# Weight-block sums of a seven-product feed-forward layer, moved from GpSimd additions to accumulating DMAs

## The chip, the cores and the metric

The kernel runs on one core of a Trainium2 chip. The metric is the device time of one execution in microseconds (us); lower is better. The engines are named PE (TensorE), ACT (ScalarE), DVE (VectorE), POOL (GpSimd) and SP (SyncE, which here issues loads).

## The reference, cut to what matters

One step of a hybrid backbone of four layers: each layer is a token mixer (short convolution, pooling, attention, short convolution) followed by a SwiGLU feed-forward part, all in float32, over 512 sample tokens and 128 prompt tokens with a model width of 1024. The part that the change touches is the feed-forward part of the last layer:

```python
D_FF = 2816
def swiglu(h, w_in, w_out):
    g, u = jnp.split(h @ w_in, 2, axis=-1)
    return (jax.nn.silu(g) * u) @ w_out
...
for i in range(DEPTH):
    ...
    hp = modulate(rms_norm(xp, norm2_w[i]), mod_p[3], mod_p[4])
    hs = modulate(rms_norm(xs, norm2_w[i]), mod_s[3], mod_s[4])
    xp = xp + mod_p[5] * swiglu(hp, ffn_in_w[i], ffn_out_w[i])
    xs = xs + mod_s[5] * swiglu(hs, ffn_in_w[i], ffn_out_w[i])
```

## The kernel before

Features lie on the 128 partitions and the 640 tokens on the free axis. Float32 products are made of three passes: a matrix is split into a high half (ACT copies it to float32r) and a low half (DVE subtracts the high half from the original), and PE adds hi x hi, hi x lo and lo x hi. Weights come in units of 128 output columns, 128 x 1024 elements (512 KB), into the four buffers `raw[:, 0..3]`. The split halves go to `w_hi` and `w_lo`, which hold two units each.

**The feed-forward part.** The 22 output tiles of `w_in` come in pairs, a gate unit and an up unit. They are worked on in three chunks of 8, 8 and 6 pairs, and behind each chunk stand two quads of units of `w_out` (the out quads). In layers 0 to 2 a pair is plain: two units, eight blocks of 128 rows of weight each. In layer 3 all pairs but the first two of the first chunk go through seven products in place of eight half-size ones, so the chunks hold 6, 8 and 6 such pairs, 20 in all. The pair is a 2 x 2 matrix of blocks: gate and up, each with the half of the weight rows that meets features 0 to 511 (here "gate half 0", "up half 0") and the half that meets the others (half 1). The tokens' 640 columns are cut into two halves too. A product is 12 matmuls (4 blocks of 128 rows x 3 passes) of 128 x 322 columns, the two extra columns carrying the shift of the modulation. The products' weight blocks, by number:

- 1: gate half 0; 2: gate half 1; 4: up half 1, as loaded
- 5: S1 = up half 0 + up half 1
- 7: S3 = gate half 0 - up half 0
- 6: S2 = S1 - gate half 0
- 3: S4 = gate half 1 - S2

Against them stand token sums T1 to T4 (`t1_hi` and so on), which POOL makes once for the layer ("turned rows"), ACT and DVE split, and all 20 pairs use. The results are added up in PSUM and by DVE (`c11`, `c12`: gate; `c21`, `c22`: up).

**What sets the order.** Each engine has one program in a fixed order with semaphores between. The products run in the order of `_order`: for pair p, product 1, then product 4 of pair p-1, then 5, 6, 2, 7, 3. `w_hi` and `w_lo` hold four blocks. When a product is done, ACT splits the block that goes to its place, four products ahead (`block_hi`, line 1250), and DVE follows (`block_lo`, line 1818). ACT also copies results out of PSUM (product 1 at line 1289, product 5 at 1296, product 6 at 1300), applies Silu (1310) and splits the hidden rows (1315). The last of a pair's blocks to be split is block 4, and its low half frees the pair's two raw buffers (line 1822, the mark). Raw buffers 0 and 1 hold even pairs, 2 and 3 odd pairs, so a pair's load begins once the pair two ahead of it is split.

**The sums before.** POOL makes the four sums of a pair with `tensor_tensor` in this order: S1 into `s1_home`, a row of `tmp` (line 591); S3 in place over up half 0, when block 1 has been split (595); S2 in place over gate half 0 (601); S4 in place over gate half 1, when block 2 has been split (608). SP's program has one loop of raw loads for the quads (`load`, line 443). The feed-forward part of layer 3 begins with one plain quad (PE lines 701 and 702; DVE line 1785 multiplies its gate and up rows), while POOL makes the turned rows.

Of the kernel before, what the change touches and what calls it, by code (L numbers as in the profile page):

```python
# [26 lines left out]
KD = D // P  # L27
# [145 lines left out]
def build(nc, d):  # L173
    with ExitStack() as ctx:
# [99 lines left out]
        s_made = sem("s_made")  # L274
# [146 lines left out]
        def _(sp):  # L421
# [58 lines left out]
            for layer in range(DEPTH):  # L480
# [33 lines left out]
                with sp.Fori(0, 2 * (Q_IN + Q_OUT)) as i:  # L514
                    load(i + q, KD)
                q += 2 * (Q_IN + Q_OUT)
                with sp.Fori(0, Q_LAST) as i:
                    load(i + q, KD)
                q += Q_LAST
# [11 lines left out]
        def _(pool):  # L531
# [45 lines left out]
            def s13(layer, c, p, q, n):  # L577

                first, j, qq = _pairs_before(layer, c), 2 * (p % 2), q + p // 2
# [3 lines left out]
                if p == 0 and c == 0:  # L583

                    pool.wait_ge(sum_ready, 2 * layer + 2)
                elif p:

                    pool.wait_ge(block_lo_ready, SEVEN * first + PLACE[n][p - 1, 5] + 1)
                elif c > FIRST_SEVEN[layer]:
                    pool.wait_ge(block_lo_ready, SEVEN * first)  # L590
                pool.tensor_tensor(s1_home, up_w[:, 0:HW], up_w[:, HW:2 * HW], ALU.add).then_inc(s_made, 1)

                pool.wait_ge(block_lo_ready, SEVEN * first + PLACE[n][p, 1] + 1)
                pool.wait_ge(s_made, 4 * (first + p) + 1)
                pool.tensor_tensor(up_w[:, 0:HW], gate_w[:, 0:HW], up_w[:, 0:HW], ALU.subtract).then_inc(s_made, 1)

            def s2(layer, c, p):
                first, gate_w = _pairs_before(layer, c), raw[:, 2 * (p % 2), :]

                pool.wait_ge(s_made, 4 * (first + p) + 2)  # L600
                pool.tensor_tensor(gate_w[:, 0:HW], s1_home, gate_w[:, 0:HW], ALU.subtract).then_inc(s_made, 1)

            def s4(layer, c, p, n):
                first, gate_w = _pairs_before(layer, c), raw[:, 2 * (p % 2), :]

                pool.wait_ge(block_lo_ready, SEVEN * first + PLACE[n][p, 2] + 1)
                pool.wait_ge(s_made, 4 * (first + p) + 3)
                pool.tensor_tensor(gate_w[:, HW:2 * HW], gate_w[:, HW:2 * HW], gate_w[:, 0:HW], ALU.subtract).then_inc(s_made, 1)

            def begin_chunk(layer, c, q, n):  # L610

                s13(layer, c, 0, q, n)
                s2(layer, c, 0)
                s4(layer, c, 0, n)

            def rest_of_chunk(layer, c, q, n, triples):

                for p in range(1, n):
                    if p % 2 == 1 and p > 1 and p // 2 < len(triples):
# [12 lines left out]
            for layer in range(DEPTH):  # L632
# [34 lines left out]
                for c in range(FIRST_SEVEN[layer], 3):  # L667
                    tiles = SEVENS[c]
                    qc = q + c * (Q_IN + Q_OUT) + (PLAIN_PAIRS // 2 if c == 0 else 0)
                    triples = [t0 + per * c + i for i in range(tiles // 2)] if ada and c < 2 else []  # L670
                    if layer == 0 and c == 2:
                        triples = [t0 + 2 * per]
                    begin_chunk(layer, c, qc, tiles)
                    if triples and not (kind == "attn" and c == 0):
                        ada_triple(triples[0])
                    rest_of_chunk(layer, c, qc, tiles, triples)
# [520 lines left out]
        def _(act):  # L1197
# [43 lines left out]
            def block_hi(n, b, first, q):  # L1241

                p, m = ORDER[n][b]
                if m in (1, 2):
                    act.wait_ge(raw_in[2 * (p % 2)], 16 * (q + p // 2) + 16)
                elif m == 4:
                    act.wait_ge(raw_in[2 * (p % 2) + 1], 16 * (q + p // 2) + 16)
                else:
                    act.wait_ge(s_made, 4 * (first + p) + {5: 1, 7: 2, 6: 3, 3: 4}[m])
                act.activation(block_home(w_hi, n, b), block_source(p, m), ACT.Copy).then_inc(block_hi_ready, 1)  # L1250
# [6 lines left out]
            def t1_hi_of(layer, k):  # L1257
                act.wait_ge(t1_made, HALF * LAYER_T[layer] + k + 1)
                act.activation(t1_hi[:, k, :], t2_full[:, k, :], ACT.Copy).then_inc(t_hi_ready, 1)

            def t2_hi_of(layer, k):
                act.wait_ge(t2_made, HALF * LAYER_T[layer] + k + 1)
                act.activation(t2_hi[:, k, :], t2_full[:, k, :], ACT.Copy).then_inc(t_hi_ready, 1)
# [4 lines left out]
            def t4_hi_of(layer, k):  # L1268
                act.wait_ge(t4_made, HALF * LAYER_T[layer] + k + 1)
                act.wait_ge(t_lo_ready, T_STEPS * LAYER_T[layer] + 2 * HALF + k + 1)  # L1270
                act.activation(t4_hi[:, k, :], t4_full[:, k, :], ACT.Copy).then_inc(t_hi_ready, 1)
# [422 lines left out]
        def _(dve):  # L1694
# [134 lines left out]
            def t1_lo_of(layer, k):  # L1829
                dve.wait_ge(t_hi_ready, T_STEPS * LAYER_T[layer] + k + 1)  # L1830
                dve.tensor_tensor(t1_lo[:, k, :], t2_full[:, k, :], t1_hi[:, k, :].bitcast(F32), ALU.subtract).then_inc(t_lo_ready, 1)

            def t2_lo_of(layer, k):
# [3 lines left out]
                dve.tensor_tensor(t2_lo[:, k, :], t2_full[:, k, :], t2_hi[:, k, :].bitcast(F32), ALU.subtract).then_inc(t_lo_ready, 1)  # L1837
# [5 lines left out]
            def t4_lo_of(layer, k):  # L1843
                dve.wait_ge(t_hi_ready, T_STEPS * LAYER_T[layer] + 3 * HALF + k + 1)
                dve.tensor_tensor(t4_lo[:, k, :], t4_full[:, k, :], t4_hi[:, k, :].bitcast(F32), ALU.subtract).then_inc(t_lo_ready, 1)

            def seven_chunk(layer, c, q, n, pr, g, tiles, ada):
# [49 lines left out]
                def after_p7(p):  # L1897
# [702 lines left out]
```

## Time and profile before

| | us |
|---|---|
| median of 3 runs (2642.04 to 2642.1) | 2642.05 |
| the profiled execution | 2642.6 |
| its span, first to last instruction | 2640.9 |
| PE busy (99% of the span) | 2624.2 |
| DVE busy (70%) | 1852.4 |
| ACT busy (34%) | 888.4 |
| POOL busy (10%) | 251.2 |

The busy share of PE counts a matmul from its start to its modelled end, and matmuls overlap, so 99% says that PE rarely stands still, not that it runs at its peak. The profile gives, for each idle stretch of an engine, what released it; a timeline gives instructions in order of time, and neighbours that are alike are merged. The seven-product chunks of layer 3 and the out quads between them lie from 2217 us to the end of the span.

### The profile page before, as it was taken

To read this page: it belongs to the slowest core of one execution; us is meant where nothing else is said; L and a number is where in the kernel's file an instruction comes from. 1 tells how busy PE (TensorE), PEld (TensorE's weight loads), DVE (VectorE), ACT (ScalarE), POOL (GpSimd) and SP (SyncE) were. 2 spreads that over 40 slices of the span, in tenths; PEclk is the share of its full clock that TensorE was granted. 3 is DMA by queue.
4 is the path that set the end of the run, shared out by engine and by line. 5 is a ranking of instruction groups with operands and counts; after the bars stand their busy time and mean duration, and the time that the engine had idled before them with its cause. 6 is when DMAs were issued, how large, how long until landed. Compare 5 with 4: busy or idle time off the path is not lost.

```text
span 2640.9 us, 45052 instructions
## 1 busy us (share of the span) xinstructions
PE 2624.2 (99%) x17398; PEld 2553.1 (97%) x17398; DVE 1852.4 (70%) x3097; ACT 888.4 (34%) x1330; POOL 251.2 (10%) x297
## 2 busy tenths in 40 slices
PE   9999999999999999999999999999999999999998
PEld 5999999999999999999967999999999999999998
DVE  5888778676586776846676668768465558849486
ACT  4223331222342222124675432221242234425253
POOL 0000000000000000000000000000000026224040
PEclk9999999999999999999999999999999999999999
DMA  8444435444224454522101245444222221312222
GB/s 308 146 143 139 132 127 175 130 156 143 77 77 128 152 158 127 152 71 75 56 13 73 82 126 162 149 127 152 69 82 72 72 79 49 104 57 90 86 76 77
DMA packets 85625, 295.19 MB, mean 112 GB/s; under 512 B 10112, under 2 KB 13312, under 8 KB 85248
## 3 DMA queue, kind: packets, MB, share of 16 engines
q1 hardware_dynamic: 60016, 200.74, 23.5%
q0 software_dynamic: 25488, 92.81, 11.4%
q8 instruction: 79, 1.29, 0.2%
q14 instruction: 42, 0.34, 0.0%
HBM read 290.63 MB, written 2.88 MB: 111 GB/s over the span
## 4 chain that ended last, share of the span: by engine, by line
PE 92%; DVE 4%; issue 1%; ACT 1%; DMA 1%; DVEq 0%; ACTq 0%; SPq 0%
PE ps L701 40%; PE ps L702 40%; PE ps L754 6%; PE ps_x L1000 1%; PE ps_sum L754 1%; PE ps L976 1%; DVE w_lo L1818 1%; PE ps_sum L987 1%; PE ps L1132 1%; DMA mix<-in_ada_head 1%; DVE w_lo L1698 1%; PE ps L1083 0%; PE ps L857 0%; ACT w_hi L1200 0%; DVE tmp L1913 0%
## 5 line engine op out<-in xcount | busy, mean ns | idle before, releaser
L1698 DVE TENSOR_TENSOR w_lo<-raw,w_hi 128x1024 fp32r<-128x1024 f32 (+2 forms) x319 | 382.3, 1198 | 464.8 <-ACT w_hi L1200 463.5
L1200 ACT ACTIVATE w_hi<-raw 128x1024 fp32r<-128x1024 f32 (+2 forms) x319 | 329.3, 1032 | 917.8 <-PE ps L702 905.8
L701 PE MATMUL ps<-h_hi,w_hi 128*128 128x320 f32 x1568 | 490.2, 313 | 1.2 <-DVE h_lo L2011 0.7
L702 PE MATMUL ps<-h_lo,w_hi 128*128 128x322 f32 x1568 | 488.5, 312 | 0.0
L701 PE MATMUL ps<-h_lo,w_hi 128*128 128x320 f32 x1568 | 487.3, 311 | 0.0
L702 PE MATMUL ps<-h_hi,w_lo 128*128 128x322 f32 x1568 | 487.3, 311 | 0.0
L701 PE MATMUL ps<-h_hi,w_lo 128*128 128x320 f32 x1568 | 487.0, 311 | 0.0
L702 PE MATMUL ps<-h_hi,w_hi 128*128 128x322 f32 x1568 | 486.0, 310 | 0.0
L1726 DVE CUSTOM_DVE_ANT_0 ps_x<-ada_w,cond 128x1024 f32<-128x1024 f32 x354 | 435.9, 1231 | 33.5 <-DVE tmp L1774 12.9
L701 PEld LDWEIGHTS ps<-h_hi,w_hi 128*128 128x128 f32 x1568 | 295.6, 189 | 2.4 <-DVE h_lo L2011 0.8
L702 PEld LDWEIGHTS ps<-h_hi,w_hi 128*128 128x128 f32 x1568 | 297.2, 190 | 0.6
L702 PEld LDWEIGHTS ps<-h_hi,w_lo 128*128 128x128 f32 x1568 | 297.3, 190 | 0.0
L701 PEld LDWEIGHTS ps<-h_hi,w_lo 128*128 128x128 f32 x1568 | 296.5, 189 | 0.0
L702 PEld LDWEIGHTS ps<-h_lo,w_hi 128*128 128x128 f32 x1568 | 295.6, 189 | 0.0
L701 PEld LDWEIGHTS ps<-h_lo,w_hi 128*128 128x128 f32 x1568 | 294.4, 188 | 0.0
L701 PE MATMUL ps<-g_hi,w_hi 128*128 128x320 f32 x884 | 274.3, 310 | 0.4
L702 PE MATMUL ps<-g_hi,w_lo 128*128 128x320 f32 x884 | 273.2, 309 | 0.0
L701 PE MATMUL ps<-g_hi,w_lo 128*128 128x320 f32 x884 | 273.1, 309 | 0.0
L702 PE MATMUL ps<-g_lo,w_hi 128*128 128x320 f32 x884 | 273.1, 309 | 0.0
L702 PE MATMUL ps<-g_hi,w_hi 128*128 128x320 f32 x884 | 273.1, 309 | 0.0
L701 PE MATMUL ps<-g_lo,w_hi 128*128 128x320 f32 x884 | 273.1, 309 | 0.0
L542 POOL DMA_DIRECT2D ada_w<-in_ada_w x177 | 93.6, 529 | 1730.4 <-DVE ada_raw L1726 1352.1
(237 smaller groups left out, 4090.9 us busy)
## 6 DMA issues: line engine op xcount, KB each, us to landing
raw<-in_weights SPq DMA_DIRECT2D x323, 512.0 KB, 3.5
ada_w<-in_ada_w POOLq DMA_DIRECT2D x177, 512.0 KB, 3.8
raw<-in_weights SPq DMA_DIRECT2D x32, 384.0 KB, 3.0
mix<-in_ada_head SPq DMA_DIRECT2D x16, 512.0 KB, 10.5
x<-in_x SPq DMA_DIRECT2D x8, 320.0 KB, 10.1
out_y<-mix SPq DMA_DIRECT2D x16, 160.0 KB, 1.9
mix<-in_spread SPq DMA_DIRECT2D x1, 1088.0 KB, 5.4
cond<-in_cond SPq DMA_DIRECT2D x1, 1024.0 KB, 13.6
```

The costliest lines, as they stand in the source:

```text
L542: pool.dma_start(ada_w[:, j * D:(j + 1) * D], d["ada_w"][ADA_N * qa + (j - LEAD)]).then_inc(ada_in[j], 16)
L701: pe.matmul(ps[:, 2 * slot, 0:TA], w[:, slot, ws], a(k)[:, 0:TA], start=begin, stop=end)
L702: mm = pe.matmul(ps[:, 2 * slot + 1, 0:width - TA], w[:, slot, ws], a(k)[:, TA:width], start=begin, stop=end)
L754: mm = pe.matmul(out, w[:, ws], a[:, k, :], start=begin and k == 0 and i == 0, stop=k == HALF - 1 and i == 2, skip_group_check=True)
L976: pe.matmul(out[:, 0:TS], row[:, qt * P:(qt + 1) * P], key[:, 0:TS], start=True, stop=True)
L987: mm = pe.transpose(sum_flat[:, k * P:(k + 1) * P], tmp[:, n % 2, k * P:(k + 1) * P], ident[:])
L1000: pe.matmul(ps_rot, val, of_sample[:, k, :], start=(k == 0), stop=(k == 4))
L1132: mm = pe.matmul(head_row[g % 2], cond_k[:, 2 * pair + k, :], head_w[:, n % HEAD_SLOTS, k * HEAD_W * P:(k + 1) * HEAD_W * P], start=(pair ...
L1200: act.activation(w_hi[:, j % 2, 0:tiles * P], raw[:, j, 0:tiles * P] if src is None else src, ACT.Copy).then_inc(w_hi_ready, 1)
L1698: dve.tensor_tensor(w_lo[:, j % 2, 0:tiles * P], raw[:, j, 0:tiles * P] if src is None else src, w_hi[:, j % 2, 0:tiles * P].bitcast(F32), ...
L1726: dve.tensor_tensor_reduce(ada_products, ada_w[:, j * D:(j + 1) * D], cond[:, v, :], 1.0, 0.0, ALU.mult, ALU.add, ada_raw[:, j, v:v + 1]). ...
L1818: dve.tensor_tensor(block_home(w_lo, n, b), block_source(p, m), block_home(w_hi, n, b).bitcast(F32), ALU.subtract).then_inc(block_lo_ready, 1)
```

## The change

The four sums of a pair are no longer made by POOL's arithmetic but by DMAs that POOL issues and that add their source to what lies at the destination. S1, S2 and S4 get places of their own: `s1_home` and `s2_home` in `rope` (a table that only the attention of layer 2 uses) and `s4_home` in the row of `tmp` where S1 was. SP loads each with one operand straight from the weights in DRAM (256 KB each), and POOL's DMA adds the other:

- S3 over up half 0: += gate half 0
- S1: loaded with up half 0, += up half 1
- S2: loaded with up half 1, += S3
- S4: loaded with gate half 1, += S2

A DMA of this kind only adds, so the up half is carried with the other sign. T1, T2 and T4 are negated when they are split (ACT `Identity` with scale -1, DVE a two-operation instruction), DVE multiplies the up results by -1 along with their scale, and the shift is subtracted where it was added. Gate half 0 and gate half 1 are no longer overwritten. SP's program for layer 3 is written out pair by pair: two raw loads, then the three homes, each with its waits. A home is reloaded when the low half of the block made from it has been split; S2's home also waits for S4 of the pair before, which reads it; and `s4_home` of the first pair waits for `sum_ready`, which SP waits for now and POOL did before. POOL's waits for raw loads stay; its waits for splits are replaced by waits for the homes and for S3 and S2. ACT waits for four semaphores of DMAs (which count 16 for each) where it waited for one that counted POOL's additions.

```diff
-        s1_home = tmp[:, 2, 0:HW]
+        s1_home, s2_home, s4_home = rope[:, 0, 0:HW], rope[:, 1, 0:HW], tmp[:, 2, 0:HW]
...
-            return {1: raw[:, j, 0:HW], 6: raw[:, j, 0:HW], 2: raw[:, j, HW:2 * HW], 3: raw[:, j, HW:2 * HW],
-                    7: raw[:, j + 1, 0:HW], 4: raw[:, j + 1, HW:2 * HW], 5: s1_home}[m]
+            return {1: raw[:, j, 0:HW], 2: raw[:, j, HW:2 * HW], 4: raw[:, j + 1, HW:2 * HW], 7: raw[:, j + 1, 0:HW],
+                    5: s1_home, 6: s2_home, 3: s4_home}[m]
...
+            def load_pair(layer, c, q, p):
+                first, place, j, qq = _pairs_before(layer, c), PLACE[SEVENS[c]], 2 * (p % 2), q + p // 2
+                load(qq, KD, (j, j + 1))
+                gate_w, up_w = d["weights"][4 * qq + j], d["weights"][4 * qq + j + 1]
+                def free(m):
+                    if p:
+                        sp.wait_ge(block_lo_ready, SEVEN * first + place[p - 1, m] + 1)
+                    elif first:
+                        sp.wait_ge(block_lo_ready, SEVEN * first)
+                free(5)
+                sp.dma_start(s1_home, up_w[:, 0:HW]).then_inc(s1_in, 16)
+                free(6)
+                if first + p:
+                    sp.wait_ge(s4_made, 16 * (first + p))
+                sp.dma_start(s2_home, up_w[:, HW:2 * HW]).then_inc(s2_in, 16)
+                free(3)
+                if p == 0 and c == FIRST_SEVEN[layer]:
+                    sp.wait_ge(sum_ready, 2 * layer + 2)
+                sp.dma_start(s4_home, gate_w[:, HW:2 * HW]).then_inc(s4_in, 16)
...
-            def s13(layer, c, p, q, n):
...
-                pool.tensor_tensor(s1_home, up_w[:, 0:HW], up_w[:, HW:2 * HW], ALU.add).then_inc(s_made, 1)
...
-                pool.tensor_tensor(up_w[:, 0:HW], gate_w[:, 0:HW], up_w[:, 0:HW], ALU.subtract).then_inc(s_made, 1)
...
+            def sums_of_pair(layer, c, p, q):
+                made, j, qq = 16 * (_pairs_before(layer, c) + p + 1), 2 * (p % 2), q + p // 2
+                gate_w, up_w = raw[:, j, :], raw[:, j + 1, :]
                 pool.wait_ge(raw_in[j], 16 * qq + 16)
                 pool.wait_ge(raw_in[j + 1], 16 * qq + 16)
+                pool.dma_start(up_w[:, 0:HW], gate_w[:, 0:HW], accum_op=ALU.add).then_inc(s3_made, 16)
+                pool.wait_ge(s1_in, made)
+                pool.dma_start(s1_home, up_w[:, HW:2 * HW], accum_op=ALU.add).then_inc(s1_made, 16)
+                pool.wait_ge(s3_made, made)
+                pool.wait_ge(s2_in, made)
+                pool.dma_start(s2_home, up_w[:, 0:HW], accum_op=ALU.add).then_inc(s2_made, 16)
+                pool.wait_ge(s2_made, made)
+                pool.wait_ge(s4_in, made)
+                pool.dma_start(s4_home, s2_home, accum_op=ALU.add).then_inc(s4_made, 16)
...
-                act.activation(t1_hi[:, k, :], t2_full[:, k, :], ACT.Copy).then_inc(t_hi_ready, 1)
+                act.activation(t1_hi[:, k, :], t2_full[:, k, :], ACT.Identity, scale=-1.0).then_inc(t_hi_ready, 1)
...
-                    dve.tensor_tensor(up_row(p)[:, TA:T], up_row(p)[:, TA:T], rinv[:, TA:T], ALU.mult).then_inc(up_scaled, 1)
+                    dve.scalar_tensor_tensor(out=up_row(p)[:, TA:T], in0=up_row(p)[:, TA:T], scalar=-1.0, in1=rinv[:, TA:T],
+                                             op0=ALU.mult, op1=ALU.mult).then_inc(up_scaled, 1)
...
-                                                     op0=ALU.add, op1=ALU.mult)
+                                                     op0=ALU.subtract, op1=ALU.mult)
```

POOL's program at the first seven-product pair of layer 3, before: the four sums of pair 0 and the first of pair 1 (`tmp` holds S1; `raw_in0` to `raw_in3` are the raw loads).

```order
L591 TENSOR_TENSOR tmp<-raw 128x512 [waits sum_ready,raw_in1,raw_in0]
L595 TENSOR_TENSOR raw<-raw 128x512 [waits s_made,block_lo_ready]
L601 TENSOR_TENSOR raw<-tmp,raw 128x512 [waits s_made]
L608 TENSOR_TENSOR raw<-raw 128x512 [waits s_made,block_lo_ready]
L591 TENSOR_TENSOR tmp<-raw 128x512 [waits block_lo_ready,raw_in3,raw_in2]
```

The same place after: S3, S1, S2 and S4 of pair 0 and S3 of pair 1, all as DMAs.

```order
L626 DMA raw<-raw 128x512 [waits raw_in1,raw_in0]
L628 DMA rope<-raw 128x512 [waits s1_in]
L632 DMA rope<-raw 128x512 [waits s2_in,s3_made]
L636 DMA tmp<-rope 128x512 [waits s4_in,s2_made]
L626 DMA raw<-raw 128x512 [waits raw_in3,raw_in2]
```

S3 moved ahead of S1, and no sum waits for a split any more; S4 stands ahead of the next pair's S3.

SP's program where the feed-forward part of layer 3 begins, before: the loop of raw loads.

```order
L514 UNCONDITIONAL_BRANCH
L514 ISA
L443 ISA [waits w_lo_ready]
L443 DMA raw<-in_weights 128x1024
L442 REGISTER_ALU
```

SP's program after, from the first seven-product pair on: pair 0, then pair 1 (`rope` is the home of S1 and then of S2, `tmp` that of S4).

```order
L449 DMA raw<-in_weights 128x1024 [waits w_lo_ready] x2
L464 DMA rope<-in_weights 128x512
L469 DMA rope<-in_weights 128x512
L474 DMA tmp<-in_weights 128x512 [waits sum_ready]
L449 DMA raw<-in_weights 128x1024 [waits w_lo_ready] x2
L464 DMA rope<-in_weights 128x512 [waits block_lo_ready]
L469 DMA rope<-in_weights 128x512 [waits s4_made,block_lo_ready]
L474 DMA tmp<-in_weights 128x512 [waits block_lo_ready]
```

Between the raw loads of two pairs there now stand three loads that wait for splits, and one of them waits for S4 of the pair before.

## Rows read from the trace of the kernel before

**Rows 1.** PE's waits, 2040 to 2641 us: total, times, longest

```profile
PE ps L754 <- ACT tmp L1289: 2.6, 1, 2.6
...
PE ps L754 <- DVE tmp L1901: 0.5, 1, 0.5
PE ps L701 <- DVE w_lo L1698: 0.4, 1, 0.4
```

**Rows 2.** windows: length, busy of PE, PEld, DVE, ACT, POOL; clock, DMA share, GB/s

```profile
2226.00:2227.00 1.00, 1.00 (x6) 1.00 (x5) 1.00 (x3) 1.00 (x3) 0.00 (x0) 0.50 0.00 0
2235.00:2236.00 1.00, 1.00 (x9) 1.00 (x8) 1.00 (x3) 1.00 (x3) 0.00 (x0) 1.00 0.02 4
2426.10:2438.95 12.85, 12.70 (x85) 12.44 (x84) 12.78 (x18) 6.83 (x13) 5.91 (x4) 1.00 0.24 82
2438.95:2451.80 12.85, 12.77 (x87) 12.51 (x86) 12.21 (x22) 6.41 (x12) 2.90 (x2) 1.00 0.34 107
```

**Rows 3.** timeline of PE: start, length, line, output<-inputs, instructions merged, idle before

```profile
2225.47 0.90 PE L754 MATMUL ps<-turned,w_hi 128*128 128x322 f32 x2 [2.59 <-ACT tmp L1289]
...
2228.65 0.31 PE L754 MATMUL ps<-h_hi,w_hi 128*128 128x322 f32 x1
...
2234.70 0.57 PE L754 MATMUL ps<-turned,w_hi 128*128 128x322 f32 x2 [0.53 <-DVE tmp L1901]
```

**Rows 4.** timeline of DVE ahead of and in the first chunk

```profile
2207.95 1.01 DVE L1785 SCALAR_TENSOR_TENSOR tmp<-tmp,bias 128x512 f32<-128x512 f32 x2
...
2220.36 2.17 DVE L1785 SCALAR_TENSOR_TENSOR tmp<-tmp,bias 128x512 f32<-128x512 f32 x2
...
2232.48 1.77 DVE L1818 TENSOR_TENSOR w_lo<-tmp,w_hi 128x512 fp32r<-128x512 f32 x1
```

**Rows 5.** timeline of ACT, the same stretch

```profile
2210.98 0.61 ACT L1250 ACTIVATE w_hi<-tmp 128x512 fp32r<-128x512 f32 x1
...
2222.56 0.74 ACT L1212 ACTIVATE g_hi<-tmp 128x640 fp32r<-128x640 f32 x1 [3.84 <-DVE tmp L1785]
...
2225.01 0.41 ACT L1289 ACTIVATE tmp<-ps 128x320 f32<-128x320 f32 x1
```

**Rows 6.** timeline of POOL, the same stretch

```profile
2204.75 1.29 POOL L591 TENSOR_TENSOR tmp<-raw 128x512 f32<-128x512 f32 x1
...
2220.63 1.74 POOL L591 TENSOR_TENSOR tmp<-raw 128x512 f32<-128x512 f32 x1
...
2231.95 1.75 POOL L601 TENSOR_TENSOR raw<-tmp,raw 128x512 f32<-128x512 f32 x1
```

**Rows 7.** DMA issues, median us to landing (x5: 2364 to 2390 us); line 542

```profile
raw<-in_weights SPq DMA_DIRECT2D x323, 512.0 KB, 3.5
ada_w<-in_ada_w POOLq DMA_DIRECT2D x177, 512.0 KB, 3.8
...
raw<-in_weights SPq DMA_DIRECT2D x4, 256.0 KB, 2.5
...
raw<-in_weights SPq DMA_DIRECT2D x5, 512.0 KB, 4.2
...
L542 POOL DMA_DIRECT2D ada_w<-in_ada_w x177: 527/527/697, 36.4 to 1824.7; - x177
```

**Rows 8.** timelines of DVE, then ACT, in the steady part of the second chunk

```profile
2375.18 0.06 DVE L1822 MEMSET marks<- 128x1 f32 x1
...
2377.91 0.69 DVE L1818 TENSOR_TENSOR w_lo<-tmp,w_hi 128x512 fp32r<-128x512 f32 x1
...
2375.20 0.63 ACT L1250 ACTIVATE w_hi<-tmp 128x512 fp32r<-128x512 f32 x1 [1.14 <-PE ps L754]
...
2387.70 0.63 ACT L1250 ACTIVATE w_hi<-tmp 128x512 fp32r<-128x512 f32 x1 [1.14 <-PE ps L754]
2389.48 0.63 ACT L1250 ACTIVATE w_hi<-raw 128x512 fp32r<-128x512 f32 x1 [1.15 <-PE ps L754]
...
2395.36 0.63 ACT L1250 ACTIVATE w_hi<-raw 128x512 fp32r<-128x512 f32 x1 [1.10 <-POOL raw L608]
```

More of the change, by code:

```diff
@@ L273, in build @@
         t_lo_ready = sem("t_lo_ready")
-        s_made = sem("s_made")
+        s1_in = sem("s1_in")
+        s2_in = sem("s2_in")
+        s4_in = sem("s4_in")
+        s1_made = sem("s1_made")
+        s2_made = sem("s2_made")
+        s3_made = sem("s3_made")
+        s4_made = sem("s4_made")
         block_hi_ready = sem("block_hi_ready")
@@ L513, in _ @@
                 q += Q_MIX[kind]
-                with sp.Fori(0, 2 * (Q_IN + Q_OUT)) as i:
+                plain = min(FIRST_SEVEN[layer], 2) * (Q_IN + Q_OUT)
+                if FIRST_SEVEN[layer] == 0:
+                    plain += PLAIN_PAIRS // 2
+                with sp.Fori(0, plain) as i:
                     load(i + q, KD)
[L516 to L519, printed above, removed]
+                q += plain
+                for c in range(FIRST_SEVEN[layer], 3):
+                    for p in range(SEVENS[c]):
+                        load_pair(layer, c, q, p)
+                    q += SEVENS[c] // 2
+                    if c < 2:
+                        with sp.Fori(0, Q_OUT) as i:
+                            load(i + q, KD)
+                        q += Q_OUT
+                if FIRST_SEVEN[layer] == 3:
+                    with sp.Fori(0, Q_LAST) as i:
+                        load(i + q, KD)
+                    q += Q_LAST
                 with sp.Fori(0, Q_OUT) as i:
@@ L582, in s13 @@
                 pool.wait_ge(raw_in[j + 1], 16 * qq + 16)
[L583 to L590, printed above, removed]
-                pool.tensor_tensor(s1_home, up_w[:, 0:HW], up_w[:, HW:2 * HW], ALU.add).then_inc(s_made, 1)
-                pool.wait_ge(block_lo_ready, SEVEN * first + PLACE[n][p, 1] + 1)
@@ L594, in s13 @@
-                pool.wait_ge(s_made, 4 * (first + p) + 1)
-                pool.tensor_tensor(up_w[:, 0:HW], gate_w[:, 0:HW], up_w[:, 0:HW], ALU.subtract).then_inc(s_made, 1)
[L597 to L619, printed above, removed]
+                pool.dma_start(up_w[:, 0:HW], gate_w[:, 0:HW], accum_op=ALU.add).then_inc(s3_made, 16)
+                pool.wait_ge(s1_in, made)
+                pool.dma_start(s1_home, up_w[:, HW:2 * HW], accum_op=ALU.add).then_inc(s1_made, 16)
@@ new lines, in sums_of_pair, with sums_of_chunk @@
+                pool.wait_ge(s3_made, made)
[4 more added lines that the diff above has]
+                pool.dma_start(s4_home, s2_home, accum_op=ALU.add).then_inc(s4_made, 16)
+            def sums_of_chunk(layer, c, q, n, triples):
+                for p in range(n):
+                    if p % 2 == 1 and p // 2 < len(triples):
@@ L620, in rest_of_chunk @@
                         ada_triple(triples[p // 2])
-                    s13(layer, c, p, q, n)
-                    s2(layer, c, p)
-                    s4(layer, c, p, n)
+                    sums_of_pair(layer, c, p, q)
             def turn_rows(layer):
@@ L672, in _ @@
                         triples = [t0 + 2 * per]
[L673 to L676, printed above, removed]
+                    sums_of_chunk(layer, c, qc, tiles, triples)
                     if ada and c < 2:
@@ L1248, in block_hi @@
                 else:
-                    act.wait_ge(s_made, 4 * (first + p) + {5: 1, 7: 2, 6: 3, 3: 4}[m])
+                    act.wait_ge({5: s1_made, 6: s2_made, 7: s3_made, 3: s4_made}[m], 16 * (first + p + 1))
                 act.activation(block_home(w_hi, n, b), block_source(p, m), ACT.Copy).then_inc(block_hi_ready, 1)
```

17 lines of the change are left out of this document (10 added, 7 removed).

## The prediction, made before the run

> **What bounds the kernel now.** I read the page's busy shares first, then TensorE's (PE's) waits in layer 3's feed-forward part, then the other engines around each wait. PE is busy for 99% of the span, so the change can win back only the little time in which PE stands still, while nothing bounds what it can lose. In the 600 us that hold everything the change touches, PE waits for little: 2.6 us once for ScalarE (ACT) and 0.5 us once for VectorE (DVE) inside the seven-product code (line 754), and 0.4 us in the plain unit ahead of it [rows 1]. The 2.6 us wait costs more than its length: the product behind it ran at a granted clock of 0.50, that is at 1.2 instead of 2.4 GHz [rows 2], and its twelve matmuls took from 2225.47 to 2228.65, 3.18 us [rows 3], where a product takes 12.50 / 7 = 1.79 us (the hi of S1 recurs every 12.50 us, 2375.20 to 2387.70 [rows 8], and a pair is seven products). So the clock cost 1.4 us more.
>
> Why did PE wait? Product 6 of pair 0 needs the copy of product 1 that ACT makes at 2225.01 (line 1289), and ACT stood behind a DVE product that ended at 2222.5 [rows 5]. That DVE step (line 1785, two instructions) took 2.17 us; the same two took 1.01 us at 2207.95 [rows 4]. In between, GpSimd (POOL) was adding S1 of pair 1, from 2220.63 for 1.74 us [rows 6]. The same shows at the second wait: a low half (line 1818) took 1.77 us at 2232.48 against 0.69 us at 2377.91 [rows 4, 8], beside a POOL addition at 2231.95 of 1.75 us [rows 6]. DVE and POOL hold each other up.
>
> In the steady part DVE is full: 12.78 us of a 12.85 us stretch, where PE idles 0.15 us, and 0.08 us in the stretch behind [rows 2]. PE there still lives on blocks split ahead, and the loop of DVE and POOL is a little slower than PE.
>
> **What the change gives back.** All 80 additions leave POOL's compute. POOL still makes the turned rows T1 to T4 until 2204.75, where its first S1 begins now [rows 6], so what PE lost before that stays.
> - The step at line 1785: 2.17 - 1.01 = 1.16 us. Everything behind it on ACT until line 1289 is a chain, so product 6 starts 1.16 us sooner. The rest of that wait, 2.59 - 1.16 = 1.43 us, stays.
> - The clock: it fell after 2.59 us of idle time, and in the stretch behind 0.53 us of idle it reads 1.00 [rows 2, 3]. 1.43 us is nearer to 0.53 than to 2.59, so I take the clock as kept: 1.40 us. Its ends are 0 and 1.40.
> - The second wait, 0.53 us [rows 3]: the DVE step ahead of it loses 1.77 - 0.69 = 1.08 us, more than the wait. All of it: 0.53 us.
> - The thin idle time in the second chunk: 0.15 + 0.08 = 0.23 us [rows 2], gone once DVE has spare time.
> Sum: 1.16 + 1.40 + 0.53 + 0.23 = 3.32 us.
>
> **What it adds beside other work.** ACT's scaled copies replace plain ones, one for one. DVE gets eight two-operation forms for T1 and T2, four for T4 and 40 for the up half, in place of plain additions and products. A two-operation form on 128x512 plus one on 128x128 takes 1.01 us [rows 4], so these are no longer than what stands now, within about 0.1 us; they lie in a DVE that loses POOL's hindrance. SP issues 60 more loads of 256 KB, and POOL 80 accumulating DMAs. None of these is on PE's path as long as each sum is there when ACT splits it. That is the point on which all hangs, so here is its room.
>
> **The room, from the steady part.** Pair P's raw blocks may be loaded once the low half of block 4 of pair P-2 is made (the mark at 2375.18 [rows 8]). Two loads of 512 KB, 4.2 us in the median there [rows 7] and one behind the other, are in by about 2380.5. POOL then issues S3 and S1. S1's home is reloaded after the low half of S1 of P-1 (2377.91 + 0.69 = 2378.6) and in 2.5 us later, 2381.1 [rows 7, 8]. ACT wants S1 at 2387.70, S2 at 2389.48 and S4 at 2395.36 [rows 8].
> - S1: 2387.7 - 2381.1 = 6.6 us for one accumulation that runs beside S3.
> - S2 behind S3: 2389.5 - 2380.5 = 9.0 us for two, 4.5 us each. This is the tightest.
> - S4 behind both: 14.9 us for three, 5.0 us each.
> - The ring: S4 of P-1 frees S2's home, which SP reloads (2.5 us), then S2, then S4 of P. That is 2.5 + 2B for an accumulation of B us, against 12.50: B up to 5.0 us.
> A late sum makes ACT wait, and behind it stand its evacuations of PE's banks; on SP the next pair's raw loads stand behind the new wait for S4; on POOL the next pair's S3 and S1 behind the waits for S2 and S4. Below B = 4.5 us nobody waits; from 5.0 the delay adds up pair by pair. Pair 0 has room: S3 and S1 can go at 2204.75, so at 3.8 us each S1 is in by about 2209.6 (ACT splits it at 2210.98 [rows 5]) and S2 by 2212.9, before ACT's turn to split it after 2217.
>
> **What an accumulation costs.** No row shows one. From below: 256 KB land in 2.5 us from SP, and POOL's queue is 0.3 us slower than SP's for 512 KB (3.8 against 3.5), so 2.8 us [rows 7]. From above: a sum reads two operands and writes one, 768 KB of movement; 512 KB cost 1.0 us more than 256 KB, so at worst 2.8 + 2 x 1.0 = 4.8 us. I take 3.8 us, the row of POOL's own 512 KB DMA, since the two operands that are read are 512 KB. With 3.8 us nobody waits. The neighbours' loads could add to it: the engines now move 1.75 MB of loads and 1 MB of sums per pair, where rows show a share of 0.24 for 1 MB [rows 2]; counting each sum twice that is 0.24 x 3.75 = 0.90 of the DMA engines. That is full enough to be my main doubt.
>
> One rule speaks against the change. The rows show POOL issuing its 177 ada loads in 527 ns each and never over 697 [rows 7], with DVE busy for 70% of the span. The Trainium skill, page "SBUF — State Buffer", section "A bandwidth-pool intuition that's wrong (but worth ruling out)", says that a DMA issued by GpSimd can stand still while DVE holds the port through which its descriptors are written, and gives 620 ns alone against 3100 ns beside a DVE copy. By that an accumulation would be an estimated 2.5 us longer, 6.3 us, and past the ring's limit. The trace's issues do not agree with it for the DVE work in them; what stands beside the new DMAs is other DVE work.
>
> **The rivals.**
> 1. *The ring closes (slower).* If B is over 5.0 us, each pair takes 2.5 + 2B. At B = 6.0: 14.5 us, 2.0 us over, for 7 + 5 + 5 = 17 intervals of the chunks of 8, 6 and 6 pairs: 34 us. Blocks are split three products ahead, 3 x 1.79 less 1.3 us for the two halves, about 4 us of cushion in each of three chunks: 34 - 12 = 22 us, less the 3.3 gained: 2642.05 + 19 = 2661 us. For it: crowded engines, three sums in series. Against: the estimate of 3.8.
> 2. *POOL's issue is held up by DVE (slower).* Each issue waits for up to one DVE step, 2.17 us at most here [rows 4]: B = 3.8 + 2.2 = 6.0, again 2661 us. Against: the 697 ns. This is the case of the Trainium skill's page above.
> 3. *The relief does not come (no change).* The DVE steps are long for another reason, or what ends last is then ACT: first and second waits stay, 2642 us.
> 4. *The waits go altogether.* All of 2.59 + 1.40 + 0.53 + 0.23 = 4.75 us and something of the plain unit's 0.4 [rows 1], with more restart time than I counted: 2636.5 us.
>
> **How the numbers follow.** The profiled execution took 2642.6 us, with 1.7 us outside the 2640.9 us span and 0.55 us over the median of the runs; the gain is taken from the median: 2642.05 - 3.32 = 2638.7 us. Its own range, with the clock's 1.4 us lost at one end and the first wait gone at the other, is 2637.0 to 2640.5. Chances: forecast 50%; relief absent, or small waits that eat the gain (B of 4.5 to 5.0), 17%; ring 24%; held issue 5%; all waits gone 4%. A measurement of this kernel can tell 0.2%, 5.3 us, from no change. So faster is the last case alone, 0.04; slower the ring and the held issue, 0.29; the rest, 0.67, is within 0.2%. The range reaches to a B of just over 6 us, 2664 us, which leaves out some 14% above and a few below.
>
> **What would show it.** Right: the accumulations land in under 4.5 us; DVE's line 1785 step ahead of the chunk takes about 1.0 us, PE's first wait there about 1.4 us and the granted clock stays at 1.00; DVE falls well under 12 us per pair; no wait of ACT for a sum. Wrong: landings over 5 us with ACT's high halves waiting for DMAs, and chunks whose pairs take longer than 12.5 us, most of it in the chunk of eight.

## The result, and the profile after

The changed kernel took 2671.37 us in the median, against 2642.07 us for the kernel before on the same chip: a ratio of 1.011 with a 95% interval of 1.0097 to 1.0122, or 29.3 us more. The forecast was 2638.7 us, the range ended at 2664 us. The direction was that of the first rival, "the ring closes".

Line numbers have moved: PE's products of the seven-product code are line 771 (was 754), ACT's high halves line 1267 (1250), its copies of product 1 line 1306 (1289), DVE's low halves line 1835 (1818), the product step ahead of the chunk line 1802 (1785). The sums are POOL's lines 626 (S3), 628 (S1), 632 (S2) and 636 (S4), SP's home loads lines 464 (S1), 469 (S2) and 474 (S4), its weight loads line 449.

The page of the changed kernel: busy time and share of each engine, then the DMA queues (q1 is SP's, q0 POOL's) with the share of 16 engines, then the chain that ended last, by engine.

```profile
PE 2632.0 (99%) x17398; PEld 2558.6 (96%) x17398; DVE 1801.5 (67%) x3097; ACT 884.5 (33%) x1330; POOL 199.4 (7%) x297
...
q1 hardware_dynamic: 68656, 216.48, 25.1%
q0 software_dynamic: 37008, 113.79, 15.8%
...
PE 87%; DMA 6%; DVE 3%; issue 2%; ACT 2%; POOL 0%; DVEq 0%; SPq 0%; ACTq 0%; POOLq 0%
```

DVE and POOL lost some 50 us of work each, as planned. But the chain of work that ended last now holds 6% of DMA. PE's waits (total, times, longest), 2040 us to the end, say where:

```profile
PE ps L771 <- DVE w_lo L1835: 22.9, 11, 4.4
PE ps L771 <- ACT tmp L1306: 1.4, 1, 1.4
```

The second row is the first wait of before [rows 1], shorter, as forecast. The first row is new: eleven waits for a low half. All eleven stand between products 5 and 6 of a pair: PE waits for S2. Six of them, 14.4 us, lie in the chunk of eight. The stretch in the middle of the chunk of eight pairs shows it against before. Columns: length, busy time of PE, PEld, DVE, ACT and POOL, granted clock, DMA share, GB/s. The kernel before:

```profile
2380.00:2460.00 80.00, 79.78 (x536) 79.16 (x535) 76.82 (x110) 42.11 (x78) 30.83 (x21) 1.00 0.26 88
```

The changed kernel:

```profile
2380.00:2460.00 80.00, 68.91 (x440) 67.73 (x439) 48.58 (x90) 33.28 (x66) 18.10 (x21) 0.96 0.78 187
```

PE stands still for 11 of 80 us here; DVE, 96% full before, is at 61%. The DMA engines went from 0.26 to 0.78.

**How one wait comes about.** Timelines of the changed kernel (start, length, idle time before and what ended it), POOL's and SP's issues in that stretch, then ACT, DVE and PE at the end of the same sum:

```profile
2405.24 0.84 POOL L636 DMA_DIRECT2D tmp<-rope  x1 [5.03 <-DMA rope<-raw]
2405.78 1.19 POOL L626 DMA_DIRECT2D raw<-raw  x1
2406.31 1.52 POOL L628 DMA_DIRECT2D rope<-raw  x1
2413.25 0.85 POOL L632 DMA_DIRECT2D rope<-raw  x1 [5.41 <-DMA rope<-in_weights]
2419.68 0.84 POOL L636 DMA_DIRECT2D tmp<-rope  x1 [5.58 <-DMA rope<-raw]
...
2408.64 0.33 SPq L469 DMA_DIRECT2D rope<-in_weights  x1
...
2412.39 0.81 SPq L449 DMA_DIRECT2D raw<-in_weights  x2
...
2419.48 0.63 ACT L1267 ACTIVATE w_hi<-rope 128x512 fp32r<-128x512 f32 x1 [6.71 <-DMA rope<-raw]
...
2420.14 0.69 DVE L1835 TENSOR_TENSOR w_lo<-rope,w_hi 128x512 fp32r<-128x512 f32 x1 [4.26 <-ACT w_hi L1267]
...
2420.98 0.53 PE L771 MATMUL ps<-turned,w_hi 128*128 128x322 f32 x2 [1.75 <-DVE w_lo L1835]
```

Each length here runs from one issue to the issue that it releases. S4 of one pair goes out at 2405.24. It frees the S2 home, which SP reloads at 2408.64, 3.4 us later. The reload is in by 2413.25, after 4.6 us, and at that moment POOL, which had waited 5.41 us for it, issues S2. S2 is in at 2419.68, after 6.4 us. There the next S4 goes out, and ACT, DVE and PE follow one after the other; PE had stood still for 1.75 us. The three members make 3.4 + 4.6 + 6.4 = 14.4 us a pair, where PE needs 12.5 us. This is the ring of the prediction, and it is longer than a pair. The pair shown is one of the shorter ones: from the second S2 of this chunk (issued at 2363.68) to the last (2458.41) they stand 12.7 to 18.4 us apart, 15.8 us in the mean.

**What the waits cost.** The clock goes with them. The changed kernel's windows in which the granted clock is below 1.00 in its seven-product chunks:

```profile
2270.00:2295.00 25.00, 21.38 (x133) 20.90 (x132) 13.59 (x25) 10.30 (x20) 5.14 (x6) 0.93 0.75 179
...
2380.00:2400.00 20.00, 15.65 (x96) 15.41 (x95) 10.88 (x21) 7.33 (x14) 4.09 (x5) 0.91 0.73 163
...
2420.00:2440.00 20.00, 16.56 (x101) 16.36 (x102) 12.73 (x24) 9.61 (x21) 5.73 (x7) 0.91 0.77 171
...
2460.00:2480.00 20.00, 16.72 (x97) 16.48 (x96) 10.90 (x23) 6.95 (x13) 0.84 (x1) 0.83 0.45 124
...
2580.00:2600.00 20.00, 17.99 (x111) 17.76 (x110) 13.36 (x26) 10.18 (x20) 3.98 (x5) 0.91 0.85 192
```

Each holds one of the five longest waits, 2.0 to 4.4 us; part of the work behind it ran at 1.2 GHz. By these rows 0.07 x 25 + 3 x 0.09 x 20 + 0.17 x 20 = 10.6 us of clock are missing. Some of that is counted in the waits already: from 2467 to 2468 us the granted clock is 0.50 while PE is busy for 0.25 us. In finer windows PE works for 18.6 us at 1.2 GHz in these five stretches, and half of that, 9.3 us, is what the clock costs. With the 22.9 us of waits it makes 32.2 us; the gains take off 3.3, and 28.9 us remain, where 29.3 were measured.

**The gains came too.** DVE's step ahead of the chunk, PE's product behind the first wait, and the product before which the second wait stood, in the changed kernel's timelines:

```profile
2220.27 1.01 DVE L1802 SCALAR_TENSOR_TENSOR tmp<-tmp,bias 128x512 f32<-128x512 f32 x2
...
2224.23 0.56 PE L771 MATMUL ps<-turned,w_hi 128*128 128x322 f32 x2 [1.44 <-ACT tmp L1306]
...
2231.81 0.56 PE L771 MATMUL ps<-turned,w_hi 128*128 128x322 f32 x2
```

The window around the second of them:

```profile
2223.00:2227.00 4.00, 2.77 (x19) 2.77 (x20) 4.00 (x9) 4.00 (x11) 0.45 (x1) 1.00 0.49 83
```

2.17 us became 1.01, the first wait 1.44 instead of 2.59 us, the granted clock behind it 1.00 (2.4 GHz) instead of 0.50, and the second wait is gone [rows 2 to 4].

### The profile page after: what moved, and what is told of

Its sections match the earlier page's. It is cut to its first block, busy times and chain, and to the rows that moved or that the text cites. A ratio compares the mean times of both kernels' runs of the same rounds, so it can differ in the third digit from the quotient of the medians.

```text
span 2670.5 us, 44991 instructions
## 1 busy us (share of the span) xinstructions
PE 2632.0 (99%) x17398; PEld 2558.6 (96%) x17398; DVE 1801.5 (67%) x3097; ACT 884.5 (33%) x1330; POOL 199.4 (7%) x297
## 3 DMA queue, kind: packets, MB, share of 16 engines
q0 software_dynamic: 37008, 113.79, 15.8%
q8 instruction: 79, 1.29, 0.2%
## 4 chain that ended last, share of the span: by engine, by line
PE 87%; DMA 6%; DVE 3%; issue 2%; ACT 2%; POOL 0%; DVEq 0%; SPq 0%; ACTq 0%; POOLq 0%
PE ps L718 39%; PE ps L719 39%; DMA rope<-raw 2%; PE ps L771 2%; DMA rope<-in_weights 2%; PE ps_x L1017 1%; PE ps L993 1%; DMA raw<-in_weights 1%; PE ps_sum L1004 1%; PE ps L1149 1%; DMA tmp<-rope 1%; DMA mix<-in_ada_head 1%; DVE w_lo L1715 1%; PE ps_sum L771 0%; DVE w_lo L1835 0%
```

## The experiments

Two theories had to be told apart. **The ring**: one S2 home, freed by S4 and reloaded, ties each pair's S2 to the S4 before. **The load**: full DMA engines make every transfer slow, whatever waits for what. A third, POOL's issue held up by DVE, was a rival too.

**1. Is it the sums' cost at all?** Two kernels keep every instruction, wait and queue and make the sums cheaper. One sums half the columns of each block (so its sums are incomplete), the other copies instead of adding (so the blocks are not sums):

```diff
-pool.dma_start(s2_home, up_w[:, 0:HW], accum_op=ALU.add)
+pool.dma_start(s2_home[:, 0:HW // 2], up_w[:, 0:HW // 2], accum_op=ALU.add)   # half sums, all four
+pool.dma_start(s2_home, up_w[:, 0:HW])                                        # plain copies, all four
```

> Every accumulating DMA adds only the first 256 of 512 columns, so half of each sum is left out; waits, homes and loads are as in the changed kernel. Ring theory: each sum loses its share of the traffic, S2 falls from 6.4 to about 4.5 us and the reload from 4.6 to 3.6, the ring to 11.5 us, under 12.5, so 2638 to 2646 us. Full-engines theory: engine time per pair falls from 10.6 to 7.6 us, also 2638 to 2646 us; the two differ in the run with two homes, not here. Held-issue theory: the issues are as many and as long, about 2671 us.

> The four DMAs of a pair copy instead of adding (so no sum is made), same queue, shapes, homes and waits. It measures what the addition costs. If reading the destination doubles a sum's traffic, a copy costs 0.7 us of the engines where a sum costs 1.5, lands in 2.8 us alone, and the ring falls to about 11.5 us: 2638 to 2646 us. If a sum is slow for its way through the queue and not for its addition, copies land in the 5 to 6 us of the sums and the time stays near 2670 us.

Measured: 2638.66 us with half sums (ratio 0.9988, 0.9978 to 0.9997) and 2638.52 us with copies (0.9987, 0.9978 to 0.9996). Both stand at the forecast, 2638.7. The rest of the change is worth what the sum said, and all of the loss lies in what the four accumulations cost. The DMA view of 2040 to 2600 us (queue: packets, MB, share of 16 engines; issues: count, KB, median us to landing), for the changed kernel:

```profile
q0 software_dynamic: 11232, 20.45, 22.0%
...
rope<-in_weights SPq DMA_DIRECT2D x40, 256.0 KB, 4.1
rope<-raw POOLq DMA_DIRECT2D x40, 256.0 KB, 5.5
```

for the kernel with copies:

```profile
q0 software_dynamic: 6400, 20.98, 10.1%
...
rope<-in_weights SPq DMA_DIRECT2D x40, 256.0 KB, 3.5
rope<-raw POOLq DMA_DIRECT2D x40, 256.0 KB, 2.6
```

The window holds the packets of 78 sums (a 79th is issued there, but the last S2, issued at 2599.44, moves its bytes behind it: 20.45 MB are 78 times 256 KB) or of 80 copies. A sum takes 0.220 x 560 / 78 = 1.58 us of all 16 engines, a copy of the same 256 KB 0.101 x 560 / 80 = 0.71 us: 2.2 times as much. In the kernel with half sums POOL's issues of S2 take 0.85 to 0.88 us, as in the changed kernel, and the time is back, so POOL's issue is not what is late. (A copy's issue takes 0.54 us.)

**2. Cut the ring, keep the bytes.** A second S2 home in a tile that is free in this layer, taken in turn; the reload then waits for S4 of the pair before the last:

```diff
-sp.wait_ge(s4_made, 16 * (first + p))
-sp.dma_start(s2_home, up_w[:, HW:2 * HW]).then_inc(s2_in, 16)
+sp.wait_ge(s4_made, 16 * (first + p - 1))
+sp.dma_start(s2_homes[p % 2], up_w[:, HW:2 * HW]).then_inc(s2_in[p % 2], 16)
```

> S2 gets two homes, one for even and one for odd pairs (the second in the modulation-weight buffer, idle in layer 3); its reload waits for S4 of the pair two before instead of the pair before. Nothing else is changed, the same bytes move. Ring theory (S4 of a pair, 3.4 us, then the reload of S2's home, 4.6 us, then S2, 6.4 us: 14.4 us against 12.5 us per pair): the ring is cut, PE's waits for late S2 go, the time falls to 2638 to 2643 us. Full-engines theory (a sum costs 1.5 us of all 16 DMA engines, with the loads 10.6 us per pair of 12.5, and what is full stays full): the bytes are the same, S2 still ends late, 2660 us or more. Held-issue theory (POOL's issues wait for DVE): nothing changes, about 2671 us.

Measured: 2647.15 us, ratio 1.0021 (1.001 to 1.0031). Some 24 of the 29 us are back with every transfer still made. PE's waits, 2217 to 2640 us:

```profile
PE ps L774 <- DVE w_lo L1838: 3.5, 1, 3.5
PE ps L774 <- ACT tmp L1309: 1.4, 1, 1.4
PE ps L774 <- ACT tmp L1320: 1.2, 1, 1.2
```

Eleven waits for a low half have become one. But 8.5 us over the kernels with cheap sums stay. The two waits that are left beside the first lie at 2253 and 2553 us, at the third pair of the first chunk and the fourth of the last.

A wider cut, two homes for each of S1, S2 and S4, asks whether more lead removes this rest:

> The changed kernel with two homes for each of S1, S2 and S4, taken in turn, and all four accumulating DMAs and all home loads kept: same bytes, twice the lead for every home. Theory A, the bytes: the DMA engines still carry 10.6 us of each 12.5 us pair, transfers still land after 4 to 6 us, and more lead for the loads removes only part: 2641 to 2650 us, about as with two S2 homes alone (2647.15 us). Rival B, lead is all that lacks: the loads run one pair ahead, every sum is made early, and the time is the 2638.5 us of the kernels with cheap sums.

Measured: 2648.18 us, ratio 1.0029 (1.002 to 1.0039). It does not. Loading homes earlier gave nothing more here once the ring was cut.

**3. Move the meeting.** In the ring, the next pair's 1 MB of weights (2412.39) goes out just ahead of S2 (2413.25). Was that meeting the cause? The loads were put behind S2 of the pair before, in the kernel with one S2 home:

```diff
+if first + p:
+    sp.wait_ge(s2_made, 16 * (first + p))
 load(qq, KD, (j, j + 1))
```

and, with two homes, behind S2 of the second pair before.

> The changed kernel, one S2 home and the ring as they are, all bytes and all sums as they are; the only edit: the two 512-KB weight loads of a pair wait until S2 of the pair before has landed, so that they no longer run beside it (in the changed kernel they start within 1 us of S2's issue in each pair of the ring, and S2 then takes 6.4 us). Theory A, this meeting of two transfers is what stretches the ring: S2 lands after 3.3 to 4 us, the loads meet S4 instead, which then takes longer than its 3.4 us but is in the ring too; the period falls from 14.4 us by about 2 us to at most 12.5 us, and the time to 2640 to 2652 us. Rival B, the engines carry a fixed sum of work in a period and what S2 gains S4 and the reload lose: 2662 to 2675 us. Rival C, the weights come too late for S3 of the next pair, and the ring grows a longer way round: over 2675 us.

> The variant with two S2 homes (2647.15 us), with one more edit: the two 512-KB weight loads of a pair wait until S2 of the second pair before has landed, since in its profile S2 took 8.2 us where 1 MB of weights was issued 1.2 us ahead of it. Theory A, the meeting of the weight loads with S2 makes what is left over the 2638.5 us of the kernels with cheap sums: the waits of 1.3 and 3.7 us on TensorE go, 2638.5 to 2642 us. Rival B, the sums that start a chunk are late by the order of their own chain, and the loads only move to another meeting: 2645 to 2650 us.

Measured: 2670.49 us (1.009 to 1.0121) with one home, 2647.29 us (1.0011 to 1.0029) with two. Neither moved: my theory fell, and each time lies in the range of rival B. Timelines of POOL and SP in the kernel with one home:

```profile
2387.05 0.85 POOL L638 DMA_DIRECT2D tmp<-rope  x1 [2.72 <-DMA rope<-raw]
...
2398.41 0.85 POOL L634 DMA_DIRECT2D rope<-raw  x1 [1.61 <-DMA rope<-in_weights]
2402.14 0.85 POOL L638 DMA_DIRECT2D tmp<-rope  x1 [2.88 <-DMA rope<-raw]
...
2386.78 0.81 SPq L449 DMA_DIRECT2D raw<-in_weights  x2
...
2395.58 0.33 SPq L471 DMA_DIRECT2D rope<-in_weights  x1
```

S2 now takes 2402.14 - 2398.41 = 3.7 us and the reload 2.8 us. But S4, which meets the weights instead, takes 2395.58 - 2387.05 = 8.5 us until SP can reload. The sum is 15.0 us, no shorter than 14.4: the part of the ring that the loads meet grew by what the others lost. PE's waits moved with it, from S2's low half to a copy of ACT (line 1319), which stands behind ACT's split of S4:

```profile
PE ps L773 <- ACT tmp L1319: 21.4, 9, 3.9
```

The kernel with two homes and later weight loads shows that full engines alone do not stop PE in the chunk of eight. Its window, columns as above:

```profile
2380.00:2460.00 80.00, 80.00 (x540) 80.00 (x539) 60.20 (x113) 41.84 (x82) 17.89 (x21) 1.00 0.85 218
```

DMA share 0.85, more than the 0.78 of the changed kernel, and PE never waits in this stretch. With two homes alone the share there is 0.79, and PE does not wait either. It takes both: a load that stretches transfers, and a ring that lets PE feel the stretch each time.

**4. Take one sum off the DMA engines.** With S1 made by one addition on POOL (from the two blocks of raw, ahead of S3), or with S4 made so (behind S2, into its home), the same transfers go: one home load and one accumulation a pair. S4 is a member of the ring, S1 is not.

```diff
-pool.dma_start(s1_home, up_w[:, HW:2 * HW], accum_op=ALU.add).then_inc(s1_made, 16)
+pool.tensor_tensor(s1_home, up_w[:, 0:HW], up_w[:, HW:2 * HW], ALU.add).then_inc(s1_made, 1)   # S1 on POOL
-pool.dma_start(s4_home, s2_home, accum_op=ALU.add).then_inc(s4_made, 16)
+pool.tensor_tensor(s4_home, gate_w[:, HW:2 * HW], s2_home, ALU.add).then_inc(s4_made, 1)       # S4 on POOL
```

> The changed kernel with its one S2 home (the ring S4, reload of the S2 home, S2, S4 stands), but S1 of each pair made by one addition on GpSimd again instead of a home load and an accumulating DMA. The four accumulations of a pair become three, and one home load of 256 KB goes: DMA engine time per pair falls from about 10.6 us to 10.6 - 1.5 - 0.7 = 8.4 us of 12.5 us. Theory A, the ring is what makes the time and full DMA engines are what stretch it past 12.5 us: with the engines at about 0.67 the members come back toward what they take alone (reload 3, S2 4, S4 3.4 us, sum 10.4 us), the period falls under 12.5 us and the time to 2638 to 2644 us. Rival B, the ring is too long whatever the load, because the order of the queues alone makes it so: the time stays at 2660 to 2672 us. GpSimd's addition (1.3 to 1.75 us a pair) holds nothing, since the ring leaves it idle; if it again slows VectorE's two-input steps as in the kernel before, one wait of about 1.5 us comes back.

> Both cuts together: two S2 homes taken in turn (no ring from S4 of one pair to S2 of the next) and S1 by one addition on GpSimd instead of a load and an accumulating DMA. With two S2 homes alone the kernel took 2647.15 us. Theory A, what was left there over the 2638.5 us of the kernels with cheap sums is contention of full DMA engines: at 8.4 us of engine time for each 12.5 us pair it goes, and the time is 2637.5 to 2640 us, no higher than the one-home variant of this same step. Rival B, what was left is in the order of the queues (a late S4 holds S3 of the next pair): 2643 to 2648 us.

> The changed kernel with one S2 home, but S4 of each pair made by one addition on GpSimd into its home instead of a home load and an accumulating DMA. The same bytes go as in the variant with S1 on GpSimd (2662.66 us), but here the member of the ring S4, reload, S2 that is taken off the engines is one of the ring's own, and no addition stands ahead of S3. Theory A, the time is the ring's period, and each member counts by what it takes under load: S4 falls from 3.4 to 7.5 us to 1.3 to 1.8 us, so the ring is 1.8 + 4 + 5 = 10.8 us, under the 12.5 us of a pair, and the time 2638 to 2645 us. Rival B, only the load on the engines counts: 2662 us as with S1 on GpSimd.

> The same with two S2 homes, so no ring at all, three accumulating DMAs and two home loads a pair. Theory A: 2637.5 to 2641 us, at or below the one-home variant, and the lowest of the kernels that compute the same if S4 on GpSimd (1.3 to 1.8 us, once a pair) does not slow VectorE where TensorE waits for it. Rival B: starts of chunks stay late as with two S2 homes and four accumulations: 2645 to 2648 us.

Measured, median and interval of the ratio to before:

| | one S2 home (ring) | two S2 homes |
|---|---|---|
| all four sums by DMA | 2671.37 (1.0097 to 1.0122) | 2647.15 (1.001 to 1.0031) |
| S1 on POOL | 2662.66 (1.0063 to 1.0091) | 2652.19 (1.0033 to 1.0076) |
| S4 on POOL | 2640.51 (0.9986 to 1.0004) | 2639.51 (0.9983 to 1.0001) |

S4 off the ring gives back 31 us, S1 with the same bytes saved 9. The window in the kernel with one home and S4 on POOL:

```profile
2380.00:2460.00 80.00, 80.00 (x541) 80.00 (x540) 61.41 (x107) 41.53 (x76) 18.96 (x18) 1.00 0.65 168
```

Its PE's waits, 2217 to 2640 us:

```profile
PE ps L770 <- ACT tmp L1305: 1.4, 1, 1.4
PE ps L770 <- DVE tmp L1921: 1.1, 1, 1.1
```

Its POOL's timeline, S2 and S4 of one pair:

```profile
2394.87 0.85 POOL L626 DMA_DIRECT2D rope<-raw  x1 [1.83 <-DMA raw<-raw]
...
2398.23 1.48 POOL L635 TENSOR_TENSOR tmp<-raw,rope 128x512 f32<-128x512 f32 x1 [2.50 <-DMA rope<-raw]
```

S2 takes 3.4 us, S4 1.48 us, and no wait for a low half is left. With S4 off the DMA engines the ring does no harm: a second S2 home on top is worth 1 us, within the spread. What stays over 2638.5 us in the profiled execution (2639.78 us) is 1.1 us of the second wait, back where POOL adds again beside DVE (a low half ahead of it takes 1.70 us in place of 0.68).

With S1 on POOL the theory fell. In two homes it even costs 5 us over the kernel without it, more than either range set for it. In its one-home form the ring's waits in the chunk of eight shrank to one of 3.1 us, but two long ones, 4.7 and 5.1 us, came in at the third pairs of the chunks of six, where the changed kernel has none. POOL and PE at the first of them:

```profile
2236.45 1.29 POOL L627 TENSOR_TENSOR rope<-raw 128x512 f32<-128x512 f32 x1 [6.66 <-DMA raw<-in_weights]
2238.03 0.86 POOL L629 DMA_DIRECT2D raw<-raw  x1 [0.30 <-POOL rope L627]
2243.05 0.85 POOL L633 DMA_DIRECT2D rope<-raw  x1 [4.16 <-DMA raw<-raw]
2250.08 0.85 POOL L637 DMA_DIRECT2D tmp<-rope  x1 [6.18 <-DMA rope<-raw]
...
2252.93 0.88 PE L772 MATMUL ps<-turned,w_hi 128*128 128x322 f32 x2 [4.68 <-DVE w_lo L1836]
```

The same S2 and S4 in the changed kernel:

```profile
2241.47 0.85 POOL L632 DMA_DIRECT2D rope<-raw  x1 [2.45 <-DMA raw<-raw]
2245.58 0.84 POOL L636 DMA_DIRECT2D tmp<-rope  x1 [3.26 <-DMA rope<-raw]
```

S3, the first link to S2, goes out behind the addition, and S2 1.6 us later than in the changed kernel, just behind the next pair's weight loads (2242.91; 2242.73 in the changed kernel). It takes 7.0 us in place of 4.1. At the other long wait it is the same (weight loads 2546.34, S2 2546.64, 7.3 us). So the addition's place ahead of S3 ate much of what the saved load gave; an order with the addition behind S3 was not tried.

**5. The cause of the first wait, alone.** In the kernel before, POOL's S1 of pair 1 was made to wait for DVE's last product of the plain quad, so that the two do not overlap:

```diff
+if p == 1 and c == FIRST_SEVEN[layer]:
+    pool.wait_ge(product_ready, ...)   # the last product of the plain quad
 pool.tensor_tensor(s1_home, up_w[:, 0:HW], up_w[:, HW:2 * HW], ALU.add)
```

> The kernel before with one wait more: POOL begins S1 of pair 1 of the first chunk only when DVE has ended its last product of the plain quad (the step of line 1785). Contention theory (that POOL addition lengthened the DVE step from 1.0 to 2.2 us, and PE's first wait cost its clock): the DVE step takes about 1.0 us, PE's first wait falls from 2.59 to 1.4 us, the granted clock stays at 1.00, and the time falls by 1.2 + 1.4 = 2.6 us to 2639.5 us. If the step is long for another reason: 2642 us, unchanged.

Measured: 2642.77 us, ratio 1.0002 (0.9993 to 1.0011). PE, POOL and ACT in its timelines:

```profile
2224.30 0.56 PE L756 MATMUL ps<-turned,w_hi 128*128 128x322 f32 x2 [1.55 <-ACT tmp L1291]
...
2234.03 0.85 PE L756 MATMUL ps<-turned,w_hi 128*128 128x322 f32 x2 [2.04 <-DVE tmp L1903]
...
2227.92 3.30 POOL L597 TENSOR_TENSOR raw<-raw 128x512 f32<-128x512 f32 x1 [5.11 <-DVE w_lo L1820]
...
2233.11 0.63 ACT L1252 ACTIVATE w_hi<-raw 128x512 fp32r<-128x512 f32 x1 [4.03 <-POOL raw L603]
```

The first wait fell from 2.59 to 1.55 us, so POOL's addition beside DVE was the cause of that part, and the clock behind it stayed at 1.00. But the time did not fall to 2639.5 us. POOL's next additions are as long as before (S3 3.30 us, 3.29 before), and PE's second wait ends only 0.67 us sooner (2234.70 before [rows 3]). So PE, which came sooner, waited there for 2.04 us in place of 0.53, and this time the clock fell behind the second wait (0.50 from 2235 to 2236). What one end gave the other took.

## Why the prediction was wrong, point by point

- **The gain, 3.32 us: right.** 1.16 us of DVE's step (1.01 us measured), 1.40 us of clock (1.00 granted behind 1.44 us of idle time), 0.53 us of the second wait (gone): each is in the rows of after. The fourth term, 0.23 us of thin idle time, is not shown apart. The kernels with cheap sums keep all of it and took 2638.66 and 2638.52 us for a forecast of 2638.7.
- **What the change adds beside other work: right.** The two-operation forms and 140 more issues cost nothing that the kernels with cheap sums show.
- **"What an accumulation costs ... I take 3.8 us ... With 3.8 us nobody waits": this step failed.** 2.8 and 4.8 us were bounds for a transfer that runs alone. Sums that met little took 3.3 to 3.7 us, so as such it was a good value. But most S1 and S2 meet loads. Their median landing was 5.5 us in the changed kernel, beyond my upper bound, and S2 of the pair shown took 6.4 us. I had worked out a DMA share of 0.90 (0.78 came) and called it my main doubt, but left the durations in the sum at what an idle engine gives.
- **"2.5 us for the reload": failed the same way.** It took 4.6 us in the pair shown (4.1 us in the median of the 40 home loads into `rope`). The room "B up to 5.0 us" came from 2.5 + 2B = 12.5. With 4.6 it is B up to 3.95 us, and the mean of S4 and S2 there was (3.4 + 6.4) / 2 = 4.9 us. The reserve that I saw was not there.
- **Rival 1, the ring (24%):** right in mechanism and place, and nearly in size. Its period, 14.5 us at B = 6, is close to the 14.4 us of the pair shown, and its 22 us of waiting to the 22.9 us of PE's waits. Part of this is luck: it had 2.5 + 6.0 + 6.0 us where 4.6 + 6.4 + 3.4 came, and the mean over the chunk of eight was 15.8 us. Its 2661 us was 10 us too low because it left out the clock, 9.3 us. I had costed the clock in the gain, behind one wait, and not in the loss, behind many.
- **Rival 2, held issue: refuted.** S2's 20 issues took 0.85 to 0.88 us, those queued right behind another up to 1.53 us, and with half sums the time is regained with S2's issues as long. The rule of the Trainium skill, page "SBUF — State Buffer", section "A bandwidth-pool intuition that's wrong (but worth ruling out)", has DMA issue from GpSimd stalled by DVE's copies; beside the DVE work of this kernel, mostly steps with two inputs, the rows show no such stall.
- **Rivals 3 and 4:** the relief came, so 3 is out; 1.44 us of the first wait stayed, so 4 is out.
- **The chances.** Half of the chance went to a forecast whose own text said that all hangs on one untested price. The range ended at 2664 us, a B of just over 6 us; with the clock's 9.3 us at that same B it would have held the result.

What stays open: the 8.5 us that two S2 homes leave, with waits at the third and fourth pairs of the chunks of six. More lead for the homes and later weight loads did not move it; S4 off the DMA engines did.

## What to carry to other kernels

Where transfers are chained by buffers that free each other, write the chain as a ring and add up what each member takes under the load that the change itself makes; if the sum with loaded durations is near the period, count on the ring. Then shorten the ring or cut it: one member moved to an engine that was idle, or one more buffer, gave 24 to 31 us here, while moving a collision about within the ring gave nothing. Do not expect a load saved outside the ring to help by its bytes: the same bytes were worth 31 us in one place and 9 in another, where the addition also put off the first link of the chain.

No version beat both kernels beyond the interval: the best that computes the same, two S2 homes and S4 on POOL, took 2639.51 us, at a ratio of 0.9983 to 1.0001.

## What the runs showed of the hardware that was not expected

- An accumulating DMA of 256 KB inside the on-chip buffer took 2.2 times the engine time of a copy (1.58 against 0.71 us of all 16 engines) in 144 instead of 80 packets (11232 / 78 and 6400 / 80). Landing in a crowd, it took 5.5 us against 2.6 us in the median.
- POOL's issue of such a DMA takes 0.85 us, against 0.54 us for a copy of the same shape and 0.53 us for its ada loads [rows 7].
- In the changed kernel the granted clock stayed at 1.00 behind waits of 1.44, 1.60, 1.75 and 1.99 us, and was below it in the five windows with waits of 2.01 to 4.35 us. That is no limit: with the weight loads put behind S2 (one home) it stayed at 1.00 behind 2.85 us (PE busy again from 2426.83) and fell to 0.50 soon after a wait of 1.79 us (that ended at 2253.57).
- POOL and DVE stretch each other: POOL's 20 additions of S3 took 1.29 us in the median in the kernel before, and the one beside DVE's steps at 2228.58 took 3.29 us; DVE's step took 2.17 in place of 1.01 us [rows 4].
